# Expert matrices with four neighbouring rows per partition, in two transfers per matrix: one decoder step on one core

## What is computed

```
def expert_block(args):
    e, tok = args
    xb = x_pad[tok]                                  # the tokens of expert e, gathered
    hgu = xb @ moe_w_gu[e] + moe_b_gu[e]             # 1024 x 2048
    gate, up = hgu[:, :D_EXPERT], hgu[:, D_EXPERT:]
    gate = jnp.minimum(gate, SWIGLU_LIMIT)
    up = jnp.clip(up, -SWIGLU_LIMIT, SWIGLU_LIMIT)
    act = (up + 1.0) * gate * jax.nn.sigmoid(SWIGLU_ALPHA * gate)
    return act @ moe_w_down[e] + moe_b_down[e]       # 1024 x 1024
```

## Time and profile before

| | us |
|---|---|
| median of 3 runs | 1236.35 (1234.32 to 1236.45) |
| profiled execution | 1235.94 |
| its span | 1234.2 |
| PE busy | 1174.4 |
| DVE busy | 382.1 |
| ACT busy | 280.1 |
| PE matmuls on `gu_w` in the loops (L982), busy | 428.7 |
| PE matmuls on `dn_w` (L899), busy | 219.6 |
| waits of L982 for transfers of `gu_w` | 24.1 |

### The profile page before, as it was taken

The page is one execution under the profiler, slowest core; times in us unless marked ns, Lnnn a source line. Parts: engine busy times, 40 slices in busy tenths (PEclk is TensorE's granted clock), DMA queues, the critical chain, the costliest instruction groups (busy, mean ns, idle before and its releaser), DMA issues.

```text
span 1234.2 us, 16622 instructions
## 1 busy us (share of the span) xinstructions
PE 1174.4 (95%) x6700; PEld 647.8 (52%) x6700; DVE 382.1 (31%) x722; ACT 280.1 (23%) x505; POOL 23.3 (2%) x47
## 2 busy tenths in 40 slices
PE   8999999999999999999999998999999999998995
PEld 8999889995434343435344443434343434343432
DVE  5888588753221212123212111121212121212124
ACT  5686454433201010101010110101110101010101
POOL 1000011001000000000000000000000000000000
PEclk9999999899999999998999998999999999999998
DMA  9745578976989999999999999999999999999993
GB/s 290 232 124 184 160 233 261 340 288 263 425 369 426 426 425 426 427 425 426 420 427 427 425 426 423 427 425 427 425 426 427 427 426 426 426 425 425 426 425 148
DMA packets 82509, 456.97 MB, mean 370 GB/s; under 512 B 6608, under 2 KB 45632, under 8 KB 48960
## 3 DMA queue, kind: packets, MB, share of 16 engines
q1 hardware_dynamic: 79632, 447.07, 89.1%
q0 software_dynamic: 2832, 9.28, 2.4%
HBM read 450.38 MB, written 5.95 MB: 370 GB/s over the span
## 4 chain that ended last, share of the span: by engine, by line
PE 61%; DMA 32%; DVE 4%; issue 2%; ACT 1%; SPq 0%; DVEq 0%; ACTq 0%
DMA gu_w<-in_moe_w_gu 31%; PE pool L982 22%; PE pool L899 10%; PE pool L625 5%; PE pool L626 5%; PE pool L627 5%; PE ub L856 5%; PE pool L919 1%; PE ob L930 1%; PE pool L887 1%; ACT wh L1050 1%; PE ob L993 1%; PE ub L819 1%; PE ub L993 1%; DMA dn_w<-in_w_in 1%
## 5 line engine op out<-in xcount | busy, mean ns | idle before, releaser
L982 PE MATMUL pool<-gu_w,arena 128*64 128x512 f32 x1920 | 428.7, 600 | 24.8 <-DMA gu_w<-in_moe_w_gu 24.1
L982 PEld LDWEIGHTS pool<-gu_w,arena 128*64 128x64 f32 x1920 | 137.3, 138 | 305.1 <-issue 249.8
L899 PE MATMUL pool<-dn_w,arena 128*64 128x512 f32 x992 | 219.6, 595 | 0.8 <-ACT arena L1240 0.8
L1722 DVE TENSOR_SCALAR arena<-pool 128x512 f32<-128x512 f32 x31 | 21.4, 692 | 629.1 <-PE pool L982 624.2
L625 PE MATMUL pool<-xh,wh 128*128 128x264 f32 x568 | 164.7, 290 | 1.4 <-DVE arena L1319 0.6
L627 PE MATMUL pool<-xh,wl 128*128 128x264 f32 x568 | 161.7, 285 | 0.0
L899 PEld LDWEIGHTS pool<-dn_w,arena 128*64 128x64 f32 x992 | 68.6, 137 | 130.8 <-issue 130.5
L1235 ACT ACTIVATE arena<-arena 128x512 f32<-128x512 f32 x32 | 20.2, 630 | 479.4 <-DVE arena L1722 479.4
L625 PEld LDWEIGHTS pool<-xh,wh 128*128 128x128 f32 x568 | 108.0, 190 | 8.1 <-issue 4.4
L626 PE MATMUL pool<-xl_most,wh 128*128 128x264 f32 x385 | 110.1, 286 | 0.0
L627 PEld LDWEIGHTS pool<-xh,wl 128*128 128x128 f32 x568 | 107.5, 189 | 0.0
(11 more groups left out here) (334 smaller groups left out, 785.0 us busy)
## 6 DMA issues: line engine op xcount, KB each, us to landing
gu_w<-in_moe_w_gu SPq DMA_DIRECT2D x124, 2048.0 KB, 22.3
dn_w<-in_moe_w_down SPq DMA_DIRECT2D x124, 1024.0 KB, 19.1
dn_w<-in_w_in SPq DMA_DIRECT2D x24, 1024.0 KB, 6.1
dn_w<-in_w_branch SPq DMA_DIRECT2D x8, 1024.0 KB, 5.6
gu_w<-in_moe_w_gu SPq DMA_DIRECT2D x8, 1024.0 KB, 8.5
gu_w<-in_state_gla POOLq DMA_DIRECT2D x8, 512.0 KB, 6.5
out_gla_sample<-gu_w POOLq DMA_DIRECT2D x8, 512.0 KB, 4.7
dn_w<-in_w_o SPq DMA_DIRECT2D x4, 1024.0 KB, 6.6
```

Of the source, the lines that this page charges most:

```text
L899: last = mm(DOWN[s * CAP:(s + 1) * CAP, :], act_t[:, k % 4, k // 4 * CAP:(k // 4 + 1) * CAP], block[:, s * HF:(s + 1) * HF], start=(k == 0 ...
L982: last = mm(out, xg[:, k, j * CAP:(j + 1) * CAP], gu_w[:, k, cols], start=False, stop=(k == NB - 1))
L1722: ts(gbuf, gate, LIMIT, None, ALU.min).then_inc(gclip, 1)
```

## The change

The rows of an expert's matrix are laid out with four neighbouring rows in a partition: blocks 4q to 4q+3 hold rows 512q + 4p + 0 to 3. A transfer fills four blocks, 32 KB in one piece per partition for `moe_w_gu` and 16 KB for `moe_w_down`, and there are two per matrix (`load_four`, `load_dn`). A transfer is issued when TensorE has used all four blocks that it overwrites, and TensorE waits for the four together (`gu_in[k // 4]`). Expert 0 still comes block by block, expert 1 in twos; of expert 31 the second halves come in twos, with semaphores of their own for the last two blocks (`gu_last`, `dn_last`). `gather` and `turn_act` take every fourth column as their stationary operand. The constants of the first layer norm are reordered to match.

```diff
-            def load_two(k, e):
-
-                sp.dma_start(gu_w[:, 2 * k:2 * k + 2, :], w_gu[0, bass.ds(e, 1), 2 * k * P:(2 * k + 2) * P, :]
-                             .rearrange("e (p a) n -> (e p) a n", a=2)).then_inc(gu_in[k], 16)
...
+            def four_rows(matrix, e, q):
+
+                return matrix[0, bass.ds(e, 1), 4 * q * P:(4 * q + 4) * P, :].rearrange("e (p a) n -> (e p) a n", a=4)
...
+            def load_two(k, e, done):
+
+                own = slice(k % 4, k % 4 + 2)
+                sp.dma_start(gu_w[:, k:k + 2, :], four_rows(w_gu, e, k // 4)[:, own, :]).then_inc(done, 16)
...
+            def load_four(q, e):
+
+                sp.dma_start(gu_w[:, 4 * q:4 * q + 4, :], four_rows(w_gu, e, q)).then_inc(gu_in[q], 16)
+
+            def load_dn(q, e):
+
+                sp.dma_start(dn_w[:, 4 * q:4 * q + 4, :], four_rows(w_down, e, q)).then_inc(dn_in[q], 16)
...
-                for k in range(NB // 2):
-                    sp.wait_ge(gu_used, n * NB + 2 * k + 2 - NB)
-                    load_two(k, e)
-                for k in range(NB // 2):
-                    sp.wait_ge(dn_used, n * NB + 2 * k + 2 - NB)
-                    load_dn(k, e)
+                for q in range(NB // 4):
+                    sp.wait_ge(gu_used, n * NB + 4 * q + 4 - NB)
+                    load_four(q, e)
+                for q in range(NB // 4):
+                    sp.wait_ge(dn_used, n * NB + 4 * q + 4 - NB)
+                    load_dn(q, e)
...
-                        last = mm(GATH[:, half, c * P:(c + 1) * P], ytok[0:rows, t, n // 2 * 2 * P + n % 2:(n // 2 + 1) * 2 * P:2],
+                        last = mm(GATH[:, half, c * P:(c + 1) * P], ytok[0:rows, t, n // 4 * 4 * P + n % 4:(n // 4 + 1) * 4 * P:4],
...
-                                               act_s[:, c // 2 * 2 * P + c % 2:(c // 2 + 1) * 2 * P:2], ident[:, :])
+                                               act_s[:, c:4 * P:4], ident[:, :])
...
-                    pe.wait_ge(gu_in[k // 2], 48)
+                    pe.wait_ge(gu_in[k // 4], 96)
...
-                        pe.wait_ge(gu_in[k // 2], n * 16 + 32)
+                        if final and j == 1 and k >= 6:
+                            pe.wait_ge(gu_last, 16)
+                        else:
+                            pe.wait_ge(gu_in[k // 4], n * 16 + 80)
```

More of the change, by code:

```diff
@@ L322, in build @@
         small_done = sem("small_done")
-        gu_in = [sem(f"gu_in{k}") for k in range(NB // 2)]
-        dn_in = [sem(f"dn_in{k}") for k in range(NB // 2)]
+        gu_in = [sem(f"gu_in{k}") for k in range(NB // 4)]
+        dn_in = [sem(f"dn_in{k}") for k in range(NB // 4)]
+        early_in = [sem(f"early_in{k}") for k in range(NB // 2)]
+        gu_last, dn_last = sem("gu_last"), sem("dn_last")
         gu_used, dn_used = sem("gu_used"), sem("dn_used")
@@ L405, in _, with load_first_dn, load_two_dn @@
         def _(sp):
+            def four_rows(matrix, e, q):
+                return matrix[0, bass.ds(e, 1), 4 * q * P:(4 * q + 4) * P, :].rearrange("e (p a) n -> (e p) a n", a=4)
             def load_gu(k, e):
-                rows = w_gu[0, e, k // 2 * 2 * P:(k // 2 + 1) * 2 * P, :].rearrange("(p a) n -> p a n", a=2)
-                sp.dma_start(gu_w[:, k, :], rows[:, k % 2, :]).then_inc(gu_in[k // 2], 16)
-            def load_two(k, e):
-                sp.dma_start(gu_w[:, 2 * k:2 * k + 2, :], w_gu[0, bass.ds(e, 1), 2 * k * P:(2 * k + 2) * P, :]
-                             .rearrange("e (p a) n -> (e p) a n", a=2)).then_inc(gu_in[k], 16)
-            def load_dn(k, e):
-                sp.dma_start(dn_w[:, 2 * k:2 * k + 2, :], w_down[0, bass.ds(e, 1), 2 * k * P:(2 * k + 2) * P, :]
-                             .rearrange("e (p a) n -> (e p) a n", a=2)).then_inc(dn_in[k], 16)
+                sp.dma_start(gu_w[:, k, :], four_rows(w_gu, e, k // 4)[:, k % 4, :]).then_inc(gu_in[k // 4], 16)
+            def load_first_dn(i):
+                k, own = 2 * i, slice(2 * i % 4, 2 * i % 4 + 2)
+                sp.dma_start(dn_w[:, k:k + 2, :], four_rows(w_down, 0, k // 4)[:, own, :]).then_inc(dn_in[k // 4], 16)
+            def load_two(k, e, done):
+                own = slice(k % 4, k % 4 + 2)
+                sp.dma_start(gu_w[:, k:k + 2, :], four_rows(w_gu, e, k // 4)[:, own, :]).then_inc(done, 16)
+            def load_two_dn(k, e, done):
+                own = slice(k % 4, k % 4 + 2)
+                sp.dma_start(dn_w[:, k:k + 2, :], four_rows(w_down, e, k // 4)[:, own, :]).then_inc(done, 16)
+            def load_four(q, e):
+                sp.dma_start(gu_w[:, 4 * q:4 * q + 4, :], four_rows(w_gu, e, q)).then_inc(gu_in[q], 16)
+            def load_dn(q, e):
+                sp.dma_start(dn_w[:, 4 * q:4 * q + 4, :], four_rows(w_down, e, q)).then_inc(dn_in[q], 16)
             def load_early(i):
-                sp.dma_start(early[i], w_down[0, 1, 2 * i * P:(2 * i + 2) * P, :].rearrange("(p a) n -> p a n", a=2)
-                             ).then_inc(dn_in[i], 16)
+                own = slice(2 * i % 4, 2 * i % 4 + 2)
+                sp.dma_start(early[i], four_rows(w_down, 1, i // 2)[:, own, :]).then_inc(early_in[i], 16)
             def load_x(half):
@@ L468, in _ @@
                 sp.wait_ge(w_lo, 2 * i + 2)
-                load_dn(i % 4, 0)
+                load_first_dn(i % 4)
                 if i == len(tiles) - 4:
@@ L494, in body @@
                 load(it * 2 + 2, 0 if pair is PAIRS - 1 else pair * 2 + 2)
[L496 to L502, removed]
-            at = moe_loops(sp, body)
-            load(at * 2 + 1, E - 1)
+            for k in range(0, NB, 2):
+                sp.wait_ge(gu_used, k + 2)
+                load_two(k, 1, gu_in[k // 4])
+            for q in range(NB // 4):
+                sp.wait_ge(gu_used, NB + 4 * q + 4)
+                load_four(q, 2)
+            for q in range(NB // 4):
+                sp.wait_ge(dn_used, 4 * q + 4)
+                load_dn(q, 2)
+            at = moe_loops(sp, body)
+            n = at * 2 + 1
+            sp.wait_ge(gu_used, n * NB + 4 - NB)
+            load_four(0, E - 1)
+            sp.wait_ge(gu_used, n * NB)
+            load_two(4, E - 1, gu_in[1])
+            load_two(6, E - 1, gu_last)
+            sp.wait_ge(dn_used, n * NB + 4 - NB)
+            load_dn(0, E - 1)
+            sp.wait_ge(dn_used, n * NB)
+            load_two_dn(4, E - 1, dn_in[1])
+            load_two_dn(6, E - 1, dn_last)
             sp.wait_ge(gu_used, (at * 2 + 1) * NB + 1)
@@ L887, in turn_act, with down @@
                     last = nc.tensor.transpose(ACTT[:, c * P:(c + 1) * P],
-                                               act_s[:, c // 2 * 2 * P + c % 2:(c // 2 + 1) * 2 * P:2], ident[:, :])
+                                               act_s[:, c:4 * P:4], ident[:, :])
                 last.then_inc(act_tr, 1)
-            def down(n, weights=dn_w, count=None):
+            def down(n, weights=dn_w, count=None, last_one=False):
                 pe.wait_ge(actt_ready, n + 1)
@@ L895, in down @@
                 for k in range(NB):
-                    pe.wait_ge(dn_in[k // 2], count or n * 16 + 16)
+                    if weights is early:
+                        pe.wait_ge(early_in[k // 2], 16)
+                    elif last_one and k >= 6:
+                        pe.wait_ge(dn_last, 16)
+                    else:
+                        pe.wait_ge(dn_in[k // 4], count or n * 16 + 16)
                     block = early[k // 2][:, k % 2, :] if weights is early else weights[:, k, :]
@@ L941, in first_pair @@
                 turn_weights(scat_done)
-                down(1, early, 32)
+                down(1, early)
             def amid():
@@ L1015, in body @@
                         turn_weights(scat_done)
-                    down(n)
+                    down(n, last_one=final and j == 1)
                     if final and j == 0:
@@ L1865, in channels, with in_fours @@
         return np.moveaxis(a, 1, 0)
[L1867 to L1869 removed]
+    def in_fours(a):
+        return np.ascontiguousarray(np.moveaxis(a.reshape(NB // 4, P, 4), 1, 0)).reshape(P, NB)
     tokens = np.concatenate([x["x_prompt"][0], x["x_sample"][:, 0]], axis=0)
```

7 lines of the change are left out of this document (3 added, 4 removed).

## The result

The changed kernel takes 1299.55 us (median of 4 runs, 1297.86 to 1301.69) against 1235.65 of the kernel before beside it (1234.32 to 1236.45): a ratio of 1.0524, 95% interval 1.051 to 1.0537. It is slower by 64 us; the forecast was 1292 us, in a range from 1234 to 1306. The profiled execution took 1298.79 us (span 1297.1, before 1234.2).

What follows compares the result with a forecast made beforehand. The kernel before was taken as bound by its 384 MiB stream; with step 4 PE would lead at 60.07 us a pair. That adds 55.6 us to 1235.94, 1291.5, with the median 0.4 above: 1292 us, range 1234 to 1306.

Steps and rivals of the forecast that it cites:

- Rival A: Stationary loads at step 4 bind PE, which leads throughout: 1280 to 1321 us, mostly 1283 to 1306; chance 0.52.
- Part 5, gather: Gather's stationary loads at step 4: reading takes 224 ns, above the spacing, +0.093 us for each of 48 instructions a pair.
- Part 5, the turn: Transposes of `act_s` at step 4: reading exceeds the spacing, +0.107 us for each of 8 turns a pair.
- The new wait before the second half of gu(1): At the start, PE waits for two transfers at blocks 4 and 5 of expert 1: 2.3 us.
- The middle: Between experts 9 and 10, PE's extra work of 11.3 us and 2.6 at the lower clock: 13.9 us.
- The loop change: Change of loops before expert 16: 4.2 us extra on PE and 2.4 at the lower clock, 6.6 us.
- Parts 1 to 4: Transfers without the step: gain from larger ones, losses from coarser waits at start and middle, and tail; sum +3.3 us.
- the period's gain: Stream, four transfers fewer per expert at 0.096 us each: 0.38 us an expert, 10.9 us in all.
- The tail: Last two blocks of expert 31: PE reaches them 0.6 us late and the split transfer costs 0.1; 0.7 us.
- C: Gather's spacing rises by less than 0.063 us and the stream still leads: 1242 to 1265 us; chance 0.08.
- D: The transfer queue doesn't run dry in the middle, so no hole there: 1232 us; chance 0.05.
- E: Pieces of 32 KB for `moe_w_gu` travel as two of 16 KB, so the gain halves: 1245 us; chance 0.05.

Runs made afterwards that it cites:

- twos_gather4: The kernel before with only gather's step raised from 2 to 4, transfers and turn untouched: 1304.42 us, ratio 1.0562.
- fours_gather2: The changed kernel with only gather's step put back from 4 to 2: 1238.21 us, ratio 1.0024 against the kernel before.
- twos_turn4: The kernel before with only the turn of `act_s` at step 4 instead of 2: 1235.3 us, ratio 1.0006.
- twos_gather8: The kernel before with only gather's columns at step 8 instead of 2: 1309.82 us.
- twos_gather3: The kernel before with only gather's columns at step 3 instead of 2: 1260.79 us.

## Why the prediction was right, and where it was off

**The side, the mechanism and the place were right.** Rival A held: gather's reading at step 4 is longer than its spacing, PE leads throughout, and the changes to the transfers vanish from the path. twos_gather4 shows the cause alone, fours_gather2 its absence.

**Part 5, gather: right cause, term too small.** Predicted +0.093 us an instruction, measured 0.246 - 0.131 = +0.115, by the chain (6.09 - 3.21) / 24 = +0.120. Over 48 instructions that is 5.8 us a pair (the chain's figure), not 4.5. The step that failed is the extrapolation: r was read from transposes (56 ns between step 1 and 2), and gather is a matmul. In gather, step 1 to 2 costs 4 ns and step 2 to 4 another 133. That 4r = 224 ns came near 246 is partly luck: by the same r, step 8 would have read in 448 ns, and it has a spacing of 0.255 us.

**Part 5, the turn: wrong.** Predicted +0.107 us a turn, 0.9 us a pair; measured nothing (twos_turn4, and 0.63 us in the changed kernel at the full clock). The errors in the two terms partly cancel: 4.5 + 0.9 = 5.3 predicted, 5.8 measured, and that so little is missing is luck.

**A term was left out: the lower clock.** In the changed kernel PE's clock falls within or behind the gathers of a pair. The windows of one pair, columns as above, with the clock third from the end; the last is one microsecond of the first:

```profile
460.00:465.00 5.00, 5.00 (x22) 4.58 (x21) 0.89 (x2) 0.00 (x0) 0.00 (x0) 0.70 0.99 426
465.00:470.00 5.00, 5.00 (x22) 4.88 (x21) 0.00 (x0) 1.99 (x5) 0.00 (x0) 0.84 0.99 426
...
463.00:464.00 1.00, 1.00 (x7) 1.00 (x6) 0.00 (x0) 0.00 (x0) 0.00 (x0) 0.50 1.21 524
```

0.50 is the 1.2 GHz level; 0.70 and 0.84 are means over about 3.0 and 1.6 us at it and the rest at 2.4 GHz. Ahead of the fall PE ran gather, with stationary loads at work for 4.58 of 5 us. Gather itself takes 6.09 us in the chain where the clock falls in it and 5.99 where it doesn't (654.57), so the loads set it, not the clock. What follows pays: in the chain above `L917` takes 0.85 us instead of 0.47, `L894` 0.63 instead of 0.37, and `L934` 7.30 instead of 7.02, some 0.9 us. Not every pair pays it: the one from 798.86 takes 60.3 us. So the pair: 54.75 + 5.76 + 0.9 = 61.4, predicted 60.07. Over all 14 pairs the mean is (1226.97 - 356.71 - 12.3 - 1.6) / 14 = 61.17, with the two extras below taken off. The 0.9 us left out here and the 0.9 us too many of the turn cancel as well.

**Terms that were too large.** The new wait before the second half of gu(1): 0.82 us, predicted 2.3. PE comes there at 320.8 us and not at 317.1, and the transfer lands at 321.6, 12.15 us after the first of the two was issued (309.47). Less 2 x 4.89 that leaves 2.4 us from issue to landing besides the bytes, where the prediction had 3.8. gu(2) starts at 356.71 (predicted 358.1). The middle: from the pair that begins at 540.90 us to 613.37 are 72.47, that is 11.1 over a pair (11.3), and 14.93 - 13.76 = 1.2 at the lower clock (2.6). The loop change: 1.59 us of issue and no lower clock behind it, together 1.6 over a pair (predicted 6.6). Both terms vary between runs: the gap is 1.59, 2.15 and 2.00 us in the three kernels with pairs of some 61 us (the changed one, twos_gather4, twos_gather8) and 3.3 to 3.9 in all others, and the 64 matmuls behind it take 13.75 us here, in twos_turn4 and twos_gather3, but 14.7 to 16.2 in the others. Why isn't shown, so one reading from one trace was too little for either. The sum from gu(2) on: 14 x (61.17 - 60.07) = +15.4, less 1.4, 1.6 and 5.0, is +7.4, and gu(30) does start at 1226.97 instead of 1219.6. The median is 7.5 us above the forecast. Too small a pair and too large extras cancel in part, which is luck too.

**Parts 1 to 4** could not show in the changed kernel, and fours_gather2 measured them: sum +3.3 predicted, +3.4 measured in the median and +5.1 in the profiled execution, from which the terms are read. So the agreement of the median shows the size of the sum, not each term. Of the terms, the period's gain was 0.31 and not 0.38 us (8.8 against 10.9), the price of a transfer some 0.08 us and not 0.096. It stood on 4.89 us, read once to 0.01 us, and the text's own bound (9 to 13) just misses it. The estimate by the Trainium skill's ceiling (DMA: Bandwidth & Descriptors, "Where 436 GB/s comes from"), 435.2 GB/s, had given a period of 29.21, and 29.22 was measured. The same section puts a limit near 358 GB/s on transfers from HBM; this trace moved 426, so it didn't bind here. The three measured periods fit the ceiling: 29.53, 29.37 and 29.22 us with eight, six and four transfers fall by 0.078 us a transfer, which leaves 28.90 us for an expert's 12 MiB, 435 GB/s, and not the 437 of the prediction's split. The holes were right in place and size: gu(3)'s first load at 353.82 (355.3), 7.7 us in the middle (the prediction's 56.3 - 48.6 is 7.7, not 7.6). The wait before gu(1)'s second half is 1.16 us there (2.3): the transfer landed 1.5 us earlier than counted. The tail cost 2.0 us and not 0.7, for which the prediction had no row.

**Rivals C, D and E fell.** C wanted a rise under 0.063 us, and it is 0.12. (Its bound was too high: by the spare time of 2.3 us a pair PE leads from 2.3 / 56 = 0.04 us on.) D wanted no second hole; fours_gather2 has it. E wanted half the gain: the large pieces bring 0.31 us for four transfers and 0.16 for the two of dn, in proportion, and the packets fell from 82509 to 65516, 17 thousand fewer. Halving the pieces of both matrices takes away 512 an expert, some 15 thousand in all, and only half as many if those of `moe_w_gu` were cut again; so pieces of 32 KB travel whole.

## What to carry to other kernels

A layout that widens a DMA's pieces is paid for where its rows are picked again: before it is chosen, look at what reads the other operand, and at how far that reading is from the spacing of its instructions. Here step 2 in gather's stationary loads cost only 0.007 us an instruction over step 1, and step 4 nearly doubled the spacing. Split such a change by its two matrices: the one half gains 4 us (1230.84), and the other then costs 69 (1299.55). And take the price of a step from an instruction of the same kind: a transpose and a matmul of the same columns don't pay alike. Count an engine's spare time over the whole path and not in its best stretch: 2.3 us a pair here, not 4.3.

## What the runs showed that was not expected

- Stationary loads of ordinary float32 matmuls, 128 columns: 192, 196, 261, 329 and 336 ns at step 1, 2, 3, 4 and 8. The price all but ends at step 4.
- Loads of float32 transposes: 140, 207 and 209 ns at step 1, 2 and 4, with the spacing hardly moved.
- With slow loads came a lower clock: the mean granted clock fell from 0.99 to 0.967 at step 3, 0.954 (changed kernel) and 0.949 (twos_gather4) at step 4 and 0.946 at step 8, while PE counted as busy for 97% of the span in the changed kernel.
- Instructions that the change doesn't touch can look slower: the loads of the contiguous turn of the weights rose from 143 to 231 ns in the median, since it mostly stands in the stretch at the lower clock; in a pair where the clock is up (at 666.7 us) their median is 142 ns. Compare durations only at the same granted clock.
